# The inversion's first four levels on four 32x32 diagonal blocks, spread into the 64-wide form ahead of the fifth

## What is computed

```
L = jnp.where(strict, jnp.einsum("...id,...jd->...ij", kb, k) * decay, 0.0)
sol = lax.linalg.triangular_solve(eye + L, rhs, left_side=True, lower=True, unit_diagonal=True)
u, w = sol[..., :dv], sol[..., dv:]
# RWKV-7, per time step
sa = jnp.einsum("dbhij,dbhj->dbhi", S, a_t)
S = S * w_t[..., None, :] + sa[..., :, None] * b_t[..., None, :] + v_t[..., :, None] * k_t[..., None, :]
```

## Time and profile before

| | us |
|---|---|
| median of 3 runs | 3202.61 |
| the profiled execution, its own time | 3213.13 |
| its span, first to last instruction | 3211.3 |
| TensorE busy | 3078.3 |
| VectorE busy | 2073.9 |
| ScalarE busy | 1648.5 |
| GpSimd busy | 611.8 |

### The profile page before, as it was taken

How to read it: one execution, slowest core, us unless ns; L and a number is a source line. 1 busy time by engine, 2 the same in 40 slices (tenths; PEclk the granted TensorE clock), 3 DMA queues, 4 the chain that set the end, 5 groups by cost and what they waited for, 6 DMA issues and landing times.

```text
span 3211.3 us, 56491 instructions
## 1 busy us (share of the span) xinstructions
PE 3078.3 (96%) x20863; PEld 2644.9 (82%) x20863; DVE 2073.9 (65%) x3472; ACT 1648.5 (51%) x2665; POOL 611.8 (19%) x517
## 2 busy tenths in 40 slices
PE   8999988889999999999999999888899999999998
PEld 7899777777888888888788997777688888888886
DVE  5775655676767777545568655567667777774554
ACT  5555654446555555444455556544465555544444
POOL 2000453440212221000000004434402221220000
PEclk9999998999999999999999999999999999999999
DMA  6666101114555555666556650011155655666654
GB/s 205 181 182 183 46 2 59 59 54 132 188 184 190 182 189 180 226 195 193 160 181 180 188 173 26 2 65 53 57 168 182 195 186 188 195 194 215 192 185 151
DMA packets 265227, 479.22 MB, mean 149 GB/s; under 512 B 17314, under 2 KB 81148, under 8 KB 264380
## 3 DMA queue, kind: packets, MB, share of 16 engines
q1 hardware_dynamic: 265020, 476.48, 47.2%
HBM read 474.32 MB, written 2.10 MB: 148 GB/s over the span
## 4 chain that ended last, share of the span: by engine, by line
PE 88%; DVE 7%; ACT 2%; issue 1%; DVEq 1%; POOL 0%; SPq 0%; DMA 0%; ACTq 0%; POOLq 0%
PE ps L643 87%; PE ps L647 1%; DVE wlo L1794 1%; ACT L1265 0%; DVE upair L1807 0%; DVE scores L2173 0%; POOL H L580 0%; DVE AR L2198 0%; DVE XS L1844 0%; DVE TN L1853 0%; DVE H L1826 0%; ACT whi L1265 0%; DVE TN L2219 0%; ACT XS L1265 0%; DVE rf L2233 0%
## 5 line engine op out<-in xcount | busy, mean ns | idle before, releaser
L1794 DVE TENSOR_TENSOR wlo<-ring,whi 128x1024 fp32r<-128x1024 f32 (+4 forms) x905 | 1088.0, 1219 | 689.7 <-ACT whi L1265 682.5
L643 PE MATMUL ps<-upair,whi 128*128 128x512 f32 x4032 | 1415.3, 397 | 6.3 <-DVE upair L1807 5.4
L1265 ACT ACTIVATE whi<-ring 128x1024 fp32r<-128x1024 f32 (+4 forms) x947 | 941.1, 1002 | 798.0 <-PE ps L643 762.3
L643 PE MATMUL ps<-upair,wlo 128*128 128x256 f32 x4032 | 1126.7, 279 | 0.0
L643 PEld LDWEIGHTS ps<-upair,whi 128*128 128x128 f32 x4032 | 757.9, 188 | 188.6 <-issue 6.0
L643 PEld LDWEIGHTS ps<-upair,wlo 128*128 128x128 f32 x4032 | 761.1, 189 | 0.3 <-issue 0.2
L643 PE MATMUL ps<-whi,upair 128*128 128x390 f32 (+2 forms) x1280 | 367.6, 364 | 0.0
L625 POOL TENSOR_TENSOR YB<-YB 128x1024 f32<-128x1024 f32 x22 | 125.2, 5692 | 838.1 <-DVE YB L1817 838.1
L643 PE MATMUL ps<-whi,ghi 128*128 128x512 f32 x704 | 274.4, 390 | 0.0
L643 PE MATMUL ps<-whi,glo 128*128 128x512 f32 x704 | 273.9, 389 | 0.0
L643 PE MATMUL ps<-wlo,ghi 128*128 128x512 f32 x704 | 273.9, 389 | 0.0
(11 more groups left out here) (312 smaller groups left out, 3703.7 us busy)
## 6 DMA issues: line engine op xcount, KB each, us to landing
ring<-in_w_up_dram SPq DMA_DIRECT2D x352, 512.0 KB, 3.8
ring<-in_w_down_dram SPq DMA_DIRECT2D x176, 512.0 KB, 4.3
ring<-in_w_in_dram SPq DMA_DIRECT2D x128, 384.0 KB, 3.6
ring<-in_w_out_dram SPq DMA_DIRECT2D x64, 512.0 KB, 3.7
ring<-in_w_ple_gate_dram SPq DMA_DIRECT2D x64, 512.0 KB, 4.2
ring<-in_w_in_dram SPq DMA_DIRECT2D x51, 512.0 KB, 4.5
ring<-in_w_in_dram SPq DMA_DIRECT2D x64, 390.0 KB, 3.6
ring<-in_w_in_dram SPq DMA_DIRECT2D x32, 396.0 KB, 3.6
```

The costliest lines, as they stand in the source:

```text
L643: return pe.matmul(o_, a, b, start=start, stop=stop, skip_group_check=True)
L1265: return act.activation(o_, i_, f, **kw)
L1794: v.tensor_tensor(wlo[:, slot % RING, :, 0:w], ring[:, slot % RING, :, 0:w], whi[:, slot % RING, :, 0:w].bitcast(F32), SUB).then_inc(S["lo ...
```

## The change

Levels 0 to 3 hold each matrix as its four 32x32 diagonal blocks, one in each quarter of the partitions (`QUARTERS`), over the same 32 columns: TNq, TTq and XSq are 128 partitions by 4 matrices by 32 columns, 128x128. Each 64x64 product becomes two of 32x32 in the tile of their quarter. Seeds, masked evictions, transposes and copies have half the columns; the seed's multiply goes by quarters. At level 3 the transposed result is spread into the 64-wide form: VectorE transposes to a spare place (`last_TNq`), drains, and multiplies a broadcast of it by a 0/1 mask (`placed`) into TNb; ScalarE makes TTb with two copies scaled by a 0/1 column (`parity`). Levels 4 and 5 stay. The 64-wide mask of level 4's eviction is in `lev_top`, and the fill products read `pred` where they read `lev`.

```diff
@@ -154,7 +154,11 @@
         headones = sb("headones", [P, P])
         incl = [sb(f"incl{d}", [P, P]) for d in range(2)]
         LEVELS, HB = 6, P // 2
-        lev = [sb(f"lev{d}", [P, LEVELS, HB], BF16) for d in range(2)]
+        QB = P // 4
+        lev = [sb(f"lev{d}", [P, LEVELS - 1, QB], BF16) for d in range(2)]
+        lev_top = [sb(f"lev_top{d}", [P, HB], BF16) for d in range(2)]
+        placed = sb("placed", [P, 2, QB], BF16)
+        parity = sb("parity", [P, 2])
         pred = [sb(f"pred{d}", [P, 2, P], BF16) for d in range(2)]
         centre = sb("centre", [P, P])
         one_h = sb("one_h", [P, P], BF16)
@@ -195,6 +199,8 @@
         TNb, TTb = ([TN[d][:, 2 * i:2 * i + 2, :].rearrange("p a c -> p (a c)").rearrange("p (j c) -> p j c", c=HB)
                      for d in range(2)] for i in range(2))
         XSb = [XS[d][:, 0:2, :].rearrange("p a c -> p (a c)").rearrange("p (j c) -> p j c", c=HB) for d in range(2)]
+        TNq, TTq = ([TN[d][:, 2 * i, :].rearrange("p (j c) -> p j c", c=QB) for d in range(2)] for i in range(2))
+        XSq, last_TNq = ([XS[d][:, i, :].rearrange("p (j c) -> p j c", c=QB) for d in range(2)] for i in range(2))
         AR = [at(f"AR{d}", [P, NT, 2, P], u_place + 4096 + 2048 * d) for d in range(2)]
         ARC = [AR, [at(f"odd_ar{d}", [P, NT, 2, P], odd_ar + 2048 * d) for d in range(2)]]
         KB = [at(f"KB{d}", [P, 2, T], u_place + 2048 * d) for d in range(2)]
@@ -281,6 +287,7 @@
         assert LEV == SMALL + 2 and 1 << (SMALL + 1) == 32
 
         EARLY = HALVES = (slice(0, HB), slice(HB, P))
+        QUARTERS = [slice(QB * q, QB * q + QB) for q in range(4)]
         LATE = EARLY[::-1]
 
         def bc(ap, n):
@@ -487,8 +494,20 @@
             pool.drain()
 
             for d in range(2):
+                for quarter in QUARTERS:
+                    pool.tensor_copy(lev[d][quarter, :, :], lev_full[d][quarter, 0:LEVELS - 1, quarter])
+                pool.drain()
                 for half in HALVES:
-                    pool.tensor_copy(lev[d][half, :, :], lev_full[d][half, :, half])
+                    pool.tensor_copy(lev_top[d][half, :], lev_full[d][half, LEVELS - 1, half])
+                pool.drain()
+            pool.memset(placed[:, :, :], 0.0)
+            pool.memset(parity[:, :], 0.0)
+            pool.drain()
+            for q, quarter in enumerate(QUARTERS):
+                pool.memset(placed[quarter, q % 2, :], 1.0)
+            pool.drain()
+            for q, quarter in enumerate(QUARTERS):
+                pool.memset(parity[quarter, q % 2:q % 2 + 1], 1.0)
             pool.drain().then_inc(S["masks"], 1)
 
             with pool.Fori(0, DEPTH) as L:
@@ -682,11 +701,11 @@
                         after(i)
 
             def keep_busy(bank=3):
-                mm(ps[bank][:, 0:T], one_h[:, :], lev[0][:, 0:4, :], True, True)
+                mm(ps[bank][:, 0:T], one_h[:, :], pred[0][:, :, :], True, True)
 
             def keep_quarters_busy(bank=3):
                 for half in HALVES:
-                    mm(ps[bank][half, 0:T], one_h[half, half], lev[0][half, 0:4, :], True, True)
+                    mm(ps[bank][half, 0:T], one_h[half, half], pred[0][half, :, :], True, True)
 
             def rw_norms(c, n, banks=(1, 5)):
                 pe.wait_ge(S["rw_sq"], n + 1)
@@ -739,7 +758,11 @@
                             pe.wait_ge(S["inv_tq"], m2 + (d + 1))
                         for j in range(4):
                             cols = slice(HB * j, HB * j + HB)
-                            if lv < LEV - 1:
+                            if lv < SMALL:
+                                for quarter in QUARTERS:
+                                    last = mm(ps[4 * d][quarter, QB * j:QB * j + QB], nt(d, j)[quarter, quarter], TNq[d][quarter, j, :],
+                                              True, True)
+                            elif lv < LEV - 1:
                                 for half in HALVES:
                                     last = mm(ps[4 * d][half, cols], nt(d, j)[half, half], TNb[d][half, j, :], True, True)
                             else:
@@ -760,7 +783,11 @@
                             last.then_inc(S["inv_q"], 1)
                         for j in range(4):
                             cols = slice(HB * j, HB * j + HB)
-                            if lv < LEV - 1:
+                            if lv < SMALL:
+                                for quarter in QUARTERS:
+                                    last = mm(ps[4 * d + 2][quarter, QB * j:QB * j + QB], XSq[d][quarter, j, :], TTq[d][quarter, j, :],
+                                              True, True)
+                            elif lv < LEV - 1:
                                 for half in HALVES:
                                     last = mm(ps[4 * d + 2][half, cols], XSb[d][half, j, :], TTb[d][half, j, :], True, True)
                             else:
@@ -1355,7 +1382,12 @@
                         else:
                             act.wait_ge(S["inv_t"], ml + (2 * lv + d + 1))
                         if lv < SMALL:
-                            last = a(mono(TTb[d]), ps[4 * d + 2][:, 0:2 * P], ACT.Copy)
+                            if lv < SMALL - 1:
+                                last = a(mono(TTq[d]), ps[4 * d + 2][:, 0:P], ACT.Copy)
+                            else:
+                                for k in range(2):
+                                    last = a(TTb[d][:, :, QB * k:QB * k + QB], third(ps[4 * d + 2][:, 0:P], 4), ACT.Copy,
+                                             scale=parity[:, k:k + 1])
                         elif lv == SMALL:
                             for half in HALVES:
                                 last = a(TT[d][half, :, half], third(ps[4 * d + 2][half, 0:2 * P], 4), ACT.Copy)
@@ -1828,10 +1860,10 @@
 
             def invert_start(d, nt):
                 v.drain()
-                for half in HALVES:
-                    v.tensor_tensor(TTb[d][half, :, :], nt[half, :, half], bmid(lev[1 - d][half, 0, :], 4), MUL)
+                for quarter in QUARTERS:
+                    v.tensor_tensor(TTq[d][quarter, :, :], nt[quarter, :, quarter], bmid(lev[1 - d][quarter, 0, :], 4), MUL)
                 v.drain()
-                v.transpose(mono(TNb[d]), mono(TTb[d])).then_inc(S["inv_tn1"], 1)
+                v.transpose(mono(TNq[d]), mono(TTq[d])).then_inc(S["inv_tn1"], 1)
 
             def invert(m2, between=None, before_last=None):
                 ml = v.snap(m2 * LEV)
@@ -1841,8 +1873,11 @@
                             before_last()
                         v.wait_ge(S["inv_x"], ml + (2 * lv + d + 1))
                         if lv < LEV - 1:
-                            v.tensor_tensor(XSb[d], third(ps[4 * d][:, 0:2 * P], 4), bmid(lev[d][:, lv + 1, :], 4), MUL)\
-                                .then_inc(S["inv_xs"], 1)
+                            if lv < SMALL:
+                                last = v.tensor_tensor(XSq[d], third(ps[4 * d][:, 0:P], 4), bmid(lev[d][:, lv + 1, :], 4), MUL)
+                            else:
+                                last = v.tensor_tensor(XSb[d], third(ps[4 * d][:, 0:2 * P], 4), bmid(lev_top[d][:, :], 4), MUL)
+                            last.then_inc(S["inv_xs"], 1)
                         else:
                             v.tensor_copy(mono(XSb[d][LATE[d], :, :]), ps[4 * d][LATE[d], 0:2 * P]).then_inc(S["inv_xs"], 1)
                     for d in range(2):
@@ -1850,7 +1885,14 @@
                             continue
                         v.wait_ge(S["inv_t"], ml + (2 * lv + d + 1))
                         if lv < SMALL:
-                            v.transpose(mono(TNb[d]), ps[4 * d + 2][:, 0:2 * P]).then_inc(S["inv_tn"], 1)
+                            if lv < SMALL - 1:
+                                v.transpose(mono(TNq[d]), ps[4 * d + 2][:, 0:P]).then_inc(S["inv_tn"], 1)
+                            else:
+                                v.transpose(mono(last_TNq[d]), ps[4 * d + 2][:, 0:P])
+                                v.drain()
+                                v.tensor_tensor(TNb[d].rearrange("p j (k c) -> p j k c", c=QB),
+                                                last_TNq[d].unsqueeze(2).to_broadcast([P, 4, 2, QB]),
+                                                placed[:, :, :].unsqueeze(1).to_broadcast([P, 4, 2, QB]), MUL).then_inc(S["inv_tn"], 1)
                         elif lv == SMALL:
                             for half in HALVES:
                                 last = v.tensor_copy(TT[0][half, :, half], third(ps[2][half, 0:2 * P], 4))
```

## The result

The changed kernel takes 3227.5 us (median of 20 runs, 3211.1 to 3241.3) and the kernel before 3211.0 (20 runs, 3202.2 to 3223.7): ratio 1.0055, 95% interval 1.0043 to 1.0067. It is slower by about 17 us where I forecast 24 less. The profiled execution of the changed kernel has a span of 3237.5 for 3211.3; it took 3239.3, 12 us over its kernel's median, where the profiled one of before (3213.1) was 2 over, so the two profiles differ by more than the kernels do.

The account below looks back on a forecast made before the run. TensorE was taken to bound the kernel (88% of the chain), in relay with VectorE inside inversions. First mixer 11.2 and delta net 12.9 less made 24 us, giving 3178.5, stated as 3180 us; range 3163 to 3215.

Parts of the forecast that it names:

- the part on TensorE: Inversion levels 0 to 3: 32 quarter records overlap across four tiles, so a side takes 0.21 us less.
- Side 0.25 to 0.28: One direction's x or t products in levels 0 to 3 take 0.25 to 0.28 us against 0.47.
- relay step 0.88 to 1.01: Levels 2 and 3, first mixer: side plus its VectorE operation takes 0.88 us, 1.01 with a fill, for 1.22.
- shape change: TensorE switching tile shape between fill products and quarter sides: 0.25 us back going into level 2 of the first mixer.
- First mixer, 11.2 less: Eight first-mixer inversions save 1.50 us each, 12.0, less seed and last-pair corrections: 11.2 us.
- Spread, 0.40 in the first mixer: Spreading to 64-wide form at level 3 adds 0.40 us per first-mixer inversion; bounds 0.2 and 0.8.
- In the delta net, 0.50: Spreading to 64-wide form at level 3 adds 0.50 us per delta-net inversion; bounds 0.2 and 0.8.
- Delta net, 12.9 less: Six delta-net inversions save 2.15 us each through shorter sides and VectorE operations: 12.9 us.
- Masks and fill operand at nothing: About 20 more small GpSimd mask operations once, and fills reading `pred` instead of `lev`, cost nothing.
- Rival A: Quarter records gain nothing on TensorE, a side stays at 0.47 us; 3195 to 3212, centre 3205; chance 0.14.
- Rival B: TensorE records go out no faster than now, a side costs 0.93 us; 3280 us; chance 0.14.
- Rival C: TensorE's clock falls in the first mixer's relay as products become shorter than waits; 16 us back, 3195; chance 0.10.

Follow-up runs that it names:

- stretch: Kernel before plus extra TensorE products ahead of its first wait, written out and looped; written-out 32x32 products took 27 to 29 ns a record, looped 14.3.
- paired: Changed kernel with half the quarter records, each product over two matrices' columns with the first's weights (inverses not the reference's); 0.9948 of the kernel before, 3187 us.
- psfirst: Changed kernel with the level-3 spread reordered: multiply from the accumulators first, then the block transpose from the on-chip buffer; 1.0034 of the kernel before.
- queue: Changed kernel with two ScalarE copies (partial result, weights) moved from ahead of the delta-net inversion to behind its level 0; 1.0045 of the kernel before.
- looped: Changed kernel with levels 2 and 3 of the first mixer's inversions as a two-round loop on TensorE; 1.0004 of the kernel before.
- queue_paired: The half-record kernel of paired with two ScalarE copies moved behind level 0 of the delta-net inversion; 0.9928 of the kernel before.
- spread: Kernel before with only the level-3 spread's work added: drain and multiply on VectorE, two scaled ScalarE copies for one; 1.0037 of the kernel before.
- q2: Changed kernel with quarters in levels 0 and 1 only, the spread moved to level 1; 1.0027 of the kernel before, 3218.8 us.

## Why the prediction was wrong

The step that failed is in the part on TensorE: "products of different halves start 0.01 us apart, so 29 is not the rate at which TensorE can be handed work". A single side of 32 records does run at 8 ns a record, as I took it. But I read a burst as a rate. Over more than one packet the rate is set by the fetch, 27 to 29 ns a record (stretch), and the 29 ns of the earlier trace rows that I explained by the tile's width is the tile's limit and the supply's, at nearly one value. The sum had no term for it. By paired, which halves the records, it is worth 253.1 less 223.5, 29.6 us in the first mixer, and 6.8 in the delta net (216.3 less 209.5), more than the whole forecast gain. With 245.3 and 246.7 for the same first mixer in psfirst and queue it is still 22 or 23. The loop, which leaves out no product, gives back 20.6 (looped, with two stops left).

By its other steps:
- *Side 0.25 to 0.28, relay step 0.88 to 1.01, evictions 292, transposes 317, seed +0.18:* right (0.25; 0.91; 292 and 317; seed multiplies 282 ns). The shape change took less than the 0.25 I gave it.
- *First mixer, 11.2 less:* right in kind once the supply suffices; paired has 15.2 less (14.1 by queue_paired, 224.6), although its spread costs more than I put in.
- *Spread, 0.40 in the first mixer:* mis-sized, 1.0 in spread. The traces offer two causes, which no run parts: the multiply's 0.64 us for 0.42 beside GpSimd, and the scaled ScalarE copies, 362 ns each where I had 280. I gave bounds of 0.2 and 0.8 and looked only at VectorE's queue, not at who else reads the buffer. *In the delta net, 0.50:* 0.52, right as far as one profile tells, until the inversion comes earlier.
- *Delta net, 12.9 less:* wrong also without the fetch. 1.3 in paired. I took every shorter side as time off the path, though ScalarE's copies of level 0 stood behind weights and a partial result; and behind them the multiply waits for GpSimd. In paired's six inversions TensorE is idle for 17.8 us for 2.6 before, and the clock falls with it, 0.90 for 0.93. 2.2 is what was left of the gain, no more than such sums vary.
- *Masks and fill operand at nothing:* nothing speaks against it; the first seed multiply starts at 351.4 for 351.6.
- *Rival A* (quarters gain nothing in a side) is refuted. *Rival B* is refuted for a side and right for a run of sides; its time, 3280, came from charging it everywhere. Of the two rules of the Trainium skill weighed there, the floor of 25 ns from start to start (TensorE: Matmul & The Clock Gate, Part 1) does not hold across tiles, 8 ns, and the ban on one accumulator bank for different row tiles (TensorEngine Tiling (Array Packing), Gotcha 1) shows in no run: four quarters write one bank and overlap. *Rival C:* the clock did fall, 0.92 to 0.82, but with the stops: at more idleness without them (paired) it is 0.91. I had the mechanism as a cause, and in the wrong mixer: without stops the clock falls in the delta net, where I had charged nothing for it.

Open: why the delta net is slowest with two quarter levels (q2); and how much of the 22 to 30 us is the stops themselves (some 13 us in the first mixer) and how much the clock behind them. Of the first mixer's inversions 106 us are at the lower clock in the changed kernel and 44 both before and in paired.

## What to carry to other kernels

Count instructions per microsecond, not only their durations: written-out TensorE code that needs less than some 28 ns a record (a load and a matmul) over more than a packet starves, and the profile calls it "issue" in the middle of a group; a loop gave most of it back here, and so did half as many, wider products. A side that becomes shorter pays only until the next queue: look up which copy the next product waits for and what stands ahead of it there. An added VectorE operation with two operands in the on-chip buffer is to be priced with GpSimd's work beside it.

## What the runs showed of the hardware

- TensorE's instructions come in packets of 256 (28 packets for 7168 instructions), one in 3.46 to 3.74 us (once 4.02) when it runs dry, at either clock; in the 13 stops of the changed kernel TensorE goes on 1.3 to 1.6 us behind the packet's end; a loop body of 1024 instructions is kept.
- 32x32 f32 products in four quarters go out at 8 ns a record in a side and 9.3 in a long kept loop; on 64x64 weights in two halves they take 28 to 31, with 32 or 64 columns.
- Two operands in the buffer on VectorE: 0.42 us alone, up to 2.60 beside GpSimd; one operand there, or one in the accumulators, unchanged at 445 and 424 ns.
